# Softmax mixer: the next tile's row maximum ahead of the low parts, and the division by the sum on VectorE

## What is computed

```python
log_f = jax.nn.log_sigmoid(f_lin.astype(jnp.float32) + f_bias.astype(jnp.float32))
c = jnp.cumsum(log_f.transpose(0, 2, 1), axis=-1)
for blk in range(S // FOX_BLOCK):
    start, end = blk * FOX_BLOCK, (blk + 1) * FOX_BLOCK
    qb = q[:, :, start:end]
    kb, vb = k[:, :, :end], v[:, :, :end]
    logits = jnp.einsum('bhqd,bhkd->bhqk', qb, kb).astype(jnp.float32) * scale
    logits = logits + (c[:, :, start:end, None] - c[:, :, None, :end])
    mask = k_pos[None, :] <= q_pos[:, None]
    probs = jax.nn.softmax(jnp.where(mask, logits, -jnp.inf), axis=-1)
    outs.append(jnp.einsum('bhqk,bhkd->bhqd', probs.astype(vb.dtype), vb))
```

## Time and profile before

| | |
|---|---|
| median of 3 runs | 1726.96 us (1726.82 to 1730.2) |
| the profiled execution | 1726.71 us, its span 1724.2 us |
| TensorE busy | 1633.9 us, 95% |
| TensorE weight loads | 1357.2 us, 79% |
| VectorE busy | 1072.9 us, 62% |
| ScalarE busy | 700.6 us, 41% |
| GpSimd busy | 663.2 us, 38% |
| mean granted TensorE clock | 0.991 |

### The profile page before, as it was taken

How to read it: one execution, slowest core, us unless ns; L and a number is a source line. 1 busy time by engine, 2 the same in 40 slices (tenths; PEclk the granted TensorE clock), 3 DMA queues, 4 the chain that set the end, 5 groups by cost and what they waited for, 6 DMA issues and landing times.

```text
span 1724.2 us, 21211 instructions
## 1 busy us (share of the span) xinstructions
PE 1633.9 (95%) x8016; PEld 1357.2 (79%) x8016; DVE 1072.9 (62%) x1641; ACT 700.6 (41%) x1070; POOL 663.2 (38%) x470
## 2 busy tenths in 40 slices
PE   4999999999989899999999979999999999999997
PEld 3888887877767778878878768788888888888886
DVE  7547987534555540006615568988666579966977
ACT  2144453235777760012032453354544553343332
POOL 3132122321324233333444268676556513323334
PEclk9999999999999999999999989999999999999998
DMA  8111000111010211111134443455344398868672
GB/s 273 72 50 37 25 25 25 37 38 37 9 42 25 62 50 49 49 49 49 49 122 125 144 135 125 166 201 187 135 155 168 134 312 265 266 195 243 207 220 98
DMA packets 207924, 200.77 MB, mean 116 GB/s; under 512 B 8520, under 2 KB 178760, under 8 KB 205776
## 3 DMA queue, kind: packets, MB, share of 16 engines
q1 hardware_dynamic: 204656, 188.35, 35.0%
q10 hardware_dynamic: 3168, 11.08, 1.7%
HBM read 153.23 MB, written 46.17 MB: 116 GB/s over the span
## 4 chain that ended last, share of the span: by engine, by line
PE 78%; DVE 8%; ACT 5%; issue 5%; DMA 2%; SPq 1%; POOL 1%; DVEq 0%; ACTq 0%; POOLq 0%
PE dense L831 9%; PE dense L833 9%; PE dense L835 9%; PE dense L1111 3%; PE dense L1112 3%; PE dense L1113 3%; PE dense L1191 3%; PE dense L1192 3%; PE dense L1193 3%; PE mixA L941 3%; ACT parts L1431 2%; PE mixA L1111 2%; PE mixA L1112 2%; PE mixA L1113 2%; PE mixB L1111 2%
## 5 line engine op out<-in xcount | busy, mean ns | idle before, releaser
L831 PE MATMUL dense<-parts 128*128 128x512 f32 x880 | 301.5, 412 | 13.0 <-ACT page L1303 4.2
L833 PE MATMUL dense<-parts 128*128 128x512 f32 x880 | 285.1, 394 | 0.0
L835 PE MATMUL dense<-parts 128*128 128x512 f32 x880 | 283.9, 392 | 0.0
L740 POOL CAST parts<-page 128x1024 fp32r<-128x1024 f32 x55 | 60.3, 1096 | 441.3 <-PE dense L835 335.8
L743 POOL TENSOR_TENSOR parts<-page,parts 128x512 fp32r<-128x512 f32 x134 | 190.5, 1442 | 48.0 <-ACT parts L1495 43.6
L835 PEld LDWEIGHTS dense<-parts 128*128 128x128 f32 x880 | 166.2, 189 | 37.0
L833 PEld LDWEIGHTS dense<-parts 128*128 128x128 f32 x880 | 166.0, 189 | 35.3
L831 PEld LDWEIGHTS dense<-parts 128*128 128x128 f32 x880 | 155.0, 191 | 40.7 <-issue 14.3
L805 POOL TENSOR_TENSOR parts<-page,parts 128x512 fp32r<-128x512 f32 x52 | 88.8, 1729 | 207.4 <-ACT parts L1606 207.4
L780 POOL TENSOR_TENSOR page<-page 128x512 f32<-128x512 f32 x80 | 122.7, 1534 | 64.2 <-PE dense L1113 26.4
L788 POOL TENSOR_TENSOR parts<-page,parts 128x512 fp32r<-128x512 f32 x80 | 112.9, 1414 | 57.7 <-ACT parts L1542 52.5
(11 more groups left out here) (242 smaller groups left out, 3742.0 us busy)
## 6 DMA issues: line engine op xcount, KB each, us to landing
page<-in_w_ff SPq DMA_DIRECT2D x104, 512.0 KB, 5.8
page<-act_scratch SPq DMA_DIRECT2D x56, 512.0 KB, 5.6
page<-in_w_in SPq DMA_DIRECT2D x90, 256.0 KB, 3.3
act_scratch<-page SPq DMA_DIRECT2D x16, 1024.0 KB, 4.0
act_scratch<-page SPq DMA_DIRECT2D x16, 768.0 KB, 7.0
page<-in_w_o SPq DMA_DIRECT2D x32, 256.0 KB, 3.2
h_scratch<-page ACTq DMA_DIRECT2D x8, 512.0 KB, 2.7
page<-c_scratch SPq DMA_DIRECT2D x8, 512.0 KB, 5.0
```

The lines of the kernel that those rows point to most:

```text
L831: mm(o, whi, x_, start=first, stop=False)
L833: mm(o, whi, x_, start=False, stop=False)
L835: ins = mm(o, wlo, x_, start=False, stop=last)
```

## The change

Two edits inside the loop over G, and nothing outside it. The scaling of tile G-1 by the reciprocal of its sum goes from ScalarE (behind the high part of tile G-2) to VectorE (behind the reciprocal). On VectorE the memset and the low part of tile G-2 go from ahead of the reduction of tile G to behind its negated maximum. The reciprocal loses its wait on the scaling two tiles back.

```diff
@@ scalar engine, step G @@
-                if 1 <= G < 65:
-                    g = G - 1
-                    x_ = F(PG_XP + g % 2, 0, (g % 8 + 1) * P)
-                    act.wait_ge(rinv_ready, g + 1)
-                    A(x_, x_, ACT.Identity, scale=rinv[:, g % 2, :]).then_inc(p_scaled, 1)
@@ vector engine, step G @@
                     dve.wait_ge(p_ready, g + 1)
-                    if g >= 2:
-                        dve.wait_ge(p_scaled, NHG + g - 1)
                     V.reciprocal(rinv[:, g % 2, :], psm[:, g % 4, :]).then_inc(rinv_ready, 1)
-                if 2 <= G < 66:
-                    g = G - 2
...
+                    dve.wait_ge(rinv_ready, g + 1)
+                    x_ = F(PG_XP + g % 2, 0, (g % 8 + 1) * P)
+                    V.tensor_scalar(x_, x_, rinv[:, g % 2, :], None, ALU.mult).then_inc(p_scaled, 1)
                 if G < 64:
...
                     V.tensor_scalar(nmx[:, G % 2, :], mx[:, G % 2, :], -1.0, None, ALU.mult).then_inc(nmx_ready, 1)
+                if 2 <= G < 66:
+                    g = G - 2
+                    L = (g % 8 + 1) * P
+                    if g >= 2:
+                        dve.wait_ge(pv_done, g // 2)
+                    if g % 2 == 0:
+                        V.memset(blocks[:, g % 8 + 1::16, 0:P].bitcast(F32), 0.0)
+                    dve.wait_ge(pt_done, g + 1)
+                    V.tensor_tensor(pt_part(g, True), mixB[:, 0:L].rearrange("q (j n) -> q j n", n=P),
+                                    pt_part(g, False).bitcast(F32), ALU.subtract).then_inc(pt_split, 1)
```

## The result

| | median us | runs | ratio to before, 95% |
|---|---|---|---|
| before | 1728.38 | 4, 1726.82 to 1730.2 | |
| changed | 1746.41 | 4, 1743.0 to 1748.32 | 1.0099 (1.0080 to 1.0118) |

The change costs 18 us; 16 had been forecast. The profiled execution took 1747.25 us (span 1745.4).

A forecast was written before the change was run, and what follows sets the result against it. The prediction took the mixer's ring of maximum, exponential, high part and low part as the bound. To 1726.7 us it added 10.7 for a new ring and 5.4 for GpSimd's hold: 1742.8, against the median 1743, range 1733 to 1751.

The forecast's parts named there:

- that ring: Softmax mixer before: maximum, exponential, high part, low part, next maximum, once a tile; 29.16 us a head.
- A new ring through TensorE: Mixer: low part, weighing, turn, scores, maximum, negated maximum, low part in series; 30.5 us a head, +10.7 us in all.
- GpSimd's share: Mixer: VectorE's multiplication waits for GpSimd's running instruction, 0.9 us in each of six heads, +5.4 us; bounds zero and 16.
- 5.5 + 0.8 and the 0.2 of the 1024-wide one: VectorE, us a head: low parts 5.5, memsets ahead of them 0.8, the 1024-wide low part's wait for its high part 0.2.
- 0.8 + 5.1 + 8.7 + 1.8: TensorE links, us a head: hand-over from low part 0.8, weighing 5.1, turn and scores 8.7, dense matmul to reduction 1.8.
- "about zero" margin: Step ahead of the 512-wide maximum: VectorE ready about when scores arrive, ScalarE's exponential standing behind a head's copy.
- The memset's term: VectorE, ahead of every second low part: 0.27 us less 0.07 overlap, 4 x 0.20 = 0.8 us a head.
- The multiplication: VectorE's per-row scaling, 64 times: 0.23 to 0.77 us by width, 32 us in all, beside the path.
- No difference: Rival: the links sum to about 29.2 us a head and multiplications find GpSimd idle; 1727, up to 1730 us; 8%.
- The ring without the lock: Rival: only the new ring costs time, GpSimd does not hold VectorE up; 1737.5 us, range 1734 to 1740; 22%.
- the lock at its upper bound: Rival: three multiplications a head each wait a whole GpSimd instruction, +16 us beside the ring's 10.7; 1753 us; 10%.
- The kernel that is faster because TensorE becomes the bound: Rival: mixer links sum to under 29.2 us a head; 1704 us at best, 1715 likelier; 5%.

The follow-up runs named there:

- the move alone: Kernel before with only memset and low part moved behind the row maximum on VectorE, scaling left on ScalarE: 1748.94 us, ratio 1.0104.
- the kernel with GpSimd light: Changed kernel with GpSimd's splits of heads 2 to 7 and dense chunks 27 to 33 cut to 8 columns instead of 512: 1743.53 us, ratio 1.0087.
- the scores out of the ring: Changed kernel with TensorE's step reordered to scores of tile G, turn of tile G-2, then weighing: 1724.12 us, ratio 0.9971.

## Why the prediction was right

*What bounds the kernel before, and that the change cuts that ring.* Right. The waits that named it, 58.7 and 31.2 us, fell to 18.4 and 4.7.

*A new ring through TensorE.* Right, in its links and in its sign: 51 reductions wait for scores, and the move alone brings the whole loss.

*Its length.* Forecast 30.5 us a head without GpSimd's share; the kernel with GpSimd light measured 31.09. As means over heads 2 to 7 of that trace, the ring parts into three. From the start of a reduction to the end of its negated maximum: 7.6 a head, as forecast. From there to the end of the low part: 6.6, where 5.5 + 0.8 and the 0.2 of the 1024-wide one made 6.5. From there to the next reduction, through TensorE: 17.0, where 0.8 + 5.1 + 8.7 + 1.8 made 16.4. So the under-sized part is the last. Half of it is the step ahead of the 512-wide maximum, which had been given "about zero" margin and has less than none. In the kernel with GpSimd light:

```profile
560.89 1.05 ACT L1386 CAST parts<-page 64x1024 fp32r<-64x1024 f32 x1
...
561.24 0.15 DVE L1933 TENSOR_SCALAR nmx<-mx 128x1 f32<-128x1 f32 x1
...
561.96 0.62 ACT L1425 ACTIVATE page<-page,nmx 128x384 f32<-128x384 f32 x1
...
562.72 0.71 PE L833 MATMUL dense<-parts 128*128 128x512 f32 x2
...
562.90 0.42 DVE L1918 TENSOR_SCALAR page<-page,rinv 128x384 f32<-128x384 f32 x1
...
563.24 0.68 DVE L1928 CUSTOM_DVE_ANT_0 page<-mixA,page 128x512 f32<-128x512 f32 x1
```

The scores are there at 562.72 + 0.23 = 562.95, the reduction starts 0.29 later, behind a multiplication that had to wait for ScalarE's copy (560.89 to 561.94, with the exponential behind it). In the other seven steps the reductions of heads 2 to 7 start within 0.01 of their scores. The other 0.3 is spread over TensorE's links and was not traced further.

The memset's term came out right by two errors that cancel. It does not overlap the negated maximum as had been assumed (546.19 + 0.15 to 546.34 above), 4 x 0.07 = 0.3 more; but the low parts take 5.8 a head and not 6.06, since those behind a memset are shorter than before.

*The multiplication.* Forecast 0.23 to 0.77 by shape; alone it took 0.33 to 0.75, 0.55 at the median. Beside the path in seven steps of eight, as said, while GpSimd is light; beside GpSimd the 640-wide one delays its reduction too, by 0.3 in the heads with a split.

*GpSimd.* Right in mechanism and place (the 384-wide and the 640-wide step pay, the 512-wide one has margin), too large in size: 0.7 us a head had been counted as a mean over the eight, 0.4 reached the path.

*The sum.* 10.7 + 5.4 = 16.1 was forecast and 18.6 measured by the periods: the ring 15.4 (31.09 against 29.16, x 8), GpSimd 3.2 (31.49 against 31.09, x 8). The ring was under-sized by 4.7 and GpSimd over-sized by 2.2; the second hid half of the first. That the total came so near is in part luck: the ring as it measured gives 1726.7 + 15.4 = 1742 by itself, which lies in the forecast's range too, so the time alone could not have told whether GpSimd had a share. The kernel with GpSimd light and the lengths of the multiplications told it.

*The rivals.* No difference would have taken links that sum to 29.2; they took 31.09 with GpSimd light. The ring without the lock is refuted by the multiplications that GpSimd lengthens, and the lock at its upper bound had put 16 us on them, where 3.2 were paid. The kernel that is faster because TensorE becomes the bound did not come about, and not even with the scores out of the ring: TensorE is busy 215.91 of 238 us there.

## What to carry to other kernels

When engines run a software pipeline in fixed orders, write down for each candidate order the rings of waits and sum each over a period; an instruction moved off one ring can close a longer one through an engine that the diff does not mention. The orders of two engines that feed each other have to be turned together: with scores ahead of turn on TensorE, low part behind maximum gained 2.9 us a head and low part ahead of it lost 6.3. A buffer that is single (mixB, the pages of turned probabilities) is a link of such a ring as much as a result is, so look there for what holds the next version.

## What the runs showed of the hardware

A multiplication by a per-row factor on 128x640 float32 took 0.55 us with GpSimd light and up to 1.5 beside a GpSimd TENSOR_TENSOR, and that pair of instructions took 2.79 us instead of 2.51 to 2.55. That both are held up stands in none of the rows above the prediction. The low part took less where it follows its memset at once, with the same work: 761 ns against 824 at 640 columns, 495 against 557 at 384, 228 against 291 at 128, 1049 against 1091 at 896, as means of eight in the changed kernel and in the one before. The widths that have no memset ahead of them took the same in both (256, 512, 768 and 1024 columns, within 2 ns). The cause was not tried.
